# Gate logits' chunks one place earlier between the attention tiles, and the last modulation columns in another PSUM region

## What is computed

```python
def _hybrid_mixer(u, w_in, b_gate, ..., w_proj_att, w_proj_ssm, w_out):
    proj = u @ w_in
    q, k, v, us, g_att, g_ssm = jnp.split(proj, [...], axis=-1)
    for window, dilation in PATTERNS:
        o, lse = _dilated_window_attention(q, k, v, slopes, window, dilation)
...
    y_att = o_att @ w_proj_att
    y_ssm = _s5_branch(us, ...) @ w_proj_ssm
    merged = jax.nn.sigmoid(g_att + gb_att) * y_att + jax.nn.sigmoid(g_ssm + gb_ssm) * y_ssm
    return merged @ w_out
...
        mod = c_act @ w_ada[l] + b_ada[l]
        sh1, sc1, gt1, sh2, sc2, gt2 = jnp.split(mod, 6, axis=-1)
```

## Time and profile before

| | us |
|---|---|
| median of 3 runs | 1996.53 |
| lowest, highest | 1995.04, 1999.32 |
| the profiled execution's own time | 1995.31 |
| its span, first to last instruction | 1993.6 |
| TensorE busy | 1971.0 (99% of the span) |
| VectorE busy | 1143.7 (57%) |
| GpSimd busy | 1319.6 (66%) |
| ScalarE busy | 668.1 (34%) |

### The profile page before, as it was taken

How to read it: one execution, slowest core, us unless ns; L and a number is a source line. 1 busy time by engine, 2 the same in 40 slices (tenths; PEclk the granted TensorE clock), 3 DMA queues, 4 the chain that set the end, 5 groups by cost and what they waited for, 6 DMA issues and landing times. The chain is left out here.

```text
span 1993.6 us, 26010 instructions
## 1 busy us (share of the span) xinstructions
PE 1971.0 (99%) x10105; PEld 1639.9 (82%) x10105; DVE 1143.7 (57%) x1363; ACT 668.1 (34%) x1115; POOL 1319.6 (66%) x795
## 2 busy tenths in 40 slices
PE   8999999999999999999999999999999999999998
PEld 6888888888888787888888898888788888888888
DVE  6962378767652676656575386722464554624554
ACT  5213233233421454444321145433434433211103
POOL 4647457655364459999746538877787888858650
PEclk9999999999999999999999999999999999999999
DMA  9645564563644213333664422333323323198332
GB/s 336 201 118 160 172 185 151 159 199 115 216 161 156 85 64 106 103 130 106 234 251 159 148 86 64 119 115 112 120 77 136 127 85 106 34 377 317 117 137 86
DMA packets 195979, 295.41 MB, mean 148 GB/s; under 512 B 15416, under 2 KB 147472, under 8 KB 195856
## 3 DMA queue, kind: packets, MB, share of 16 engines
q1 hardware_dynamic: 185488, 270.55, 40.4%
q10 hardware_dynamic: 10368, 23.19, 3.1%
HBM read 213.73 MB, written 79.97 MB: 147 GB/s over the span
## 5 line engine op out<-in xcount | busy, mean ns | idle before, releaser
L1668 PE MATMUL ps<-tb,w_h 128*128 128x512 f32 x1344 | 416.9, 391 | 2.5 <-DVE quads L3056 1.9
L1052 POOL TENSOR_SCALAR w_h<-raw 128x512 fp32r<-128x512 f32 (+2 forms) x100 | 225.5, 2255 | 282.8 <-issue 127.1
L1173 POOL TENSOR_TENSOR w_l<-raw,w_h 128x512 fp32r<-128x512 f32 x210 | 309.5, 1483 | 92.6 <-ACT w_h L2307 92.6
L1668 PEld LDWEIGHTS ps<-tb,w_h 128*128 128x128 f32 x1344 | 251.3, 188 | 59.2 <-issue 3.9
L1668 PE MATMUL ps<-tb,w_l 128*128 128x512 f32 x672 | 261.5, 389 | 0.0
L2307 ACT ACTIVATE w_h<-raw 128x512 fp32r<-128x512 f32 x210 | 130.8, 627 | 236.8 <-PE ps L1668 150.3
L1668 PE MATMUL ps<-act_h,w_h 128*128 128x512 f32 x504 | 196.3, 389 | 0.6 <-ACT quads L2336 0.5
L1054 POOL TENSOR_TENSOR w_l<-raw,w_h 128x512 fp32r<-128x512 f32 (+2 forms) x100 | 191.3, 1913 | 8.3
L1668 PE MATMUL ps<-act_l,w_h 128*128 128x512 f32 x504 | 196.1, 389 | 0.0
L1668 PE MATMUL ps<-act_h,w_l 128*128 128x512 f32 x504 | 196.1, 389 | 0.0
L1668 PEld LDWEIGHTS ps<-tb,w_l 128*128 128x128 f32 x672 | 126.1, 188 | 26.3
(11 more groups left out here) (455 smaller groups left out, 4581.2 us busy)
## 6 DMA issues: line engine op xcount, KB each, us to landing
raw<-in_w_in SPq DMA_DIRECT2D x44, 1024.0 KB, 5.3
raw<-in_w_up SPq DMA_DIRECT2D x16, 1024.0 KB, 5.2
f_scratch<-r SPq DMA_DIRECT2D x16, 1024.0 KB, 8.3
gates_scratch<-quads SPq DMA_DIRECT2D x24, 512.0 KB, 7.6
r<-gates_scratch SPq DMA_DIRECT2D x12, 1024.0 KB, 6.4
ada_lo<-in_w_ada SPq DMA_DIRECT2D x16, 512.0 KB, 4.1
ada_hi<-in_w_ada SPq DMA_DIRECT2D x16, 512.0 KB, 4.4
gates_scratch<-gate_st ACTq DMA_DIRECT2D x32, 256.0 KB, 3.0
```

The source lines that it names most:

```text
L1052: nc.gpsimd.tensor_scalar(w_h[:, k, c, :], src[:, c, :], 1.0, None, ALU.mult).then_inc(s["w_high"], 1)
L1173: nc.gpsimd.tensor_tensor(w7_l[:, SLOTS[o]], x, w7_h[:, SLOTS[o]].bitcast(F32), ALU.subtract)\
L1668: last = nc.tensor.matmul(bank_of(n, bank), w[:, SLOTS[o], c, :], x(c), start=(first and c == 0 and p == 0), stop=(c == KD // 2 - 1 and p ...
```

## The change

Four edits, all on the attention stage and the step behind it. No instruction is added or taken away.

1. The chunks of the gates move one place forward: chunk 0 stands before the scores of the first two tiles, every `gate_part(i)` covers chunks 4i + 1 to 4i + 4 in place of 4i to 4i + 3, and the last tile has two chunks in place of three.
2. The last pair of modulation columns is written to the first two columns of slot 2, the transposes' region (`columns_of`), and TensorE no longer waits for `o_ready` and `mod2_ready` right before it.
3. The product that overwrites slot 3 now waits for `o_ready` and for the last but one read of columns. The one that overwrites slot 2 waits for the last read.
4. DVE reads the last pair of columns behind its last `o_low`.

```diff
+        def columns_of(k):
+            return slot(2)[:, 0:2] if k == NT // 4 - 1 else slot(3)[:, 2 * P:2 * P + 2]
...
             def gate_part(i):
 
-                gate_chunks(KD // 2 * i, KD // 2 * i + KD // 2)
+                gate_chunks(KD // 2 * i + 1, KD // 2 * i + KD // 2 + 1)
...
-                ada(slot(3)[:, 2 * P:2 * P + 2], ada_parts[k % 2]).then_inc(s["ada_done"], 1)
+                ada(columns_of(k), ada_parts[k % 2]).then_inc(s["ada_done"], 1)
...
+            pe.wait_ge(s["s5_act"], S5_ACT["sig_ready"] + 1)
+            gate_chunks(0, 1)
             for t in range(2):
                 scores(t)
-            pe.wait_ge(s["s5_act"], S5_ACT["sig_ready"] + 1)
-            gate_part(0)
+            gate_chunks(1, 5)
             scores(2)
...
                 else:
-                    gate_chunks(4 * KD * KD - 12 + 3 * (t - NT + 4), 4 * KD * KD - 9 + 3 * (t - NT + 4))
+                    at_g = 4 * KD * KD - 11 + 3 * (t - NT + 4)
+                    gate_chunks(at_g, min(at_g + 3, 4 * KD * KD))
...
             def last_columns_of_modulation():
 
-                pe.wait_ge(s["o_ready"], AHEAD + NT // 2)
-                pe.wait_ge(s["mod2_ready"], NT // 4 - 1)
                 modulation_columns(NT // 4 - 1)
...
                         pe.wait_ge(s["gate_read"], AHEAD + 4 * KD)
-                        pe.wait_ge(s["mod2_ready"], NT // 4)
+                        pe.wait_ge(s["o_ready"], AHEAD + NT // 2)
+                        pe.wait_ge(s["mod2_ready"], NT // 4 - 1)
...
                 if j == 0:
                     for cg in range(2):
+                        if cg:
+                            pe.wait_ge(s["mod2_ready"], NT // 4)
                         product(slot(2 * cg), N_PROJ % 2, cg, KA, o_h, o_l, each=None if cg else s["ot_ready"]).then_inc(s["gemm"], 2)
...
-                v.tensor_tensor(mod[:, lo:lo + 2], slot(3)[:, 2 * P:2 * P + 2], col_a("b_ada", lo, 2), ALU.add)\
+                v.tensor_tensor(mod[:, lo:lo + 2], columns_of(k), col_a("b_ada", lo, 2), ALU.add)\
                  .then_inc(s["mod2_ready"], 1)
...
-            modulation_read(NT // 4 - 1)
             normalised(NT // 4 - 1)
             for c in range(2, KA):
                 o_low(c)
+            modulation_read(NT // 4 - 1)
```

## The result

The changed kernel takes 2026.55 us (median of 5 runs, 2023.81 to 2030.01) against 1996.53 us before; the ratio is 1.0154, with a 95% interval of 1.0142 to 1.0167. It is slower by 30.0 us. Forecast were 2020.5 us, in a range of 2015.5 to 2027.5: the direction and the mechanism held, the size was 6 us short. The profiled execution took 2030.01 us, with a span of 2028.3 us, so it lies 3.5 us over the median.

What follows compares the result with a forecast made beforehand. TensorE, busy 1971.0 of 1993.6 us, was taken as the bound. 1995.3 + 33.3 - 5.2 - 3.9 - 0.2 = 2019.3 us, plus 1.2 to the median gave 2020.5 us, range 2015.5 to 2027.5.

Steps and rivals of the forecast that it cites:

- The exposed hand-over, 30 x 1.11 us: Attention stage: each group's first gate matmul waits uncovered for ScalarE's read of the bank, 1.57 - 0.46 us; 33.3 us added.
- ScalarE ready in time, with 1.15 us to spare: Gate hand-overs: ScalarE's read, due 0.69 us earlier, starts at once, as 1.15 of at least 1.84 us idle time remain.
- The old waits for the bank, 5.2 us won: Attention stage: 9 + 7 earlier TensorE waits for ScalarE's gate reads go; 5.2 us won, 4.4 to 5.4.
- The waits for VectorE's copy, 3.9 us won: Attention stage: five column-matmul waits for `prob_t` go because TensorE comes later; 3.9 us won, bounds 0 to 3.9.
- The start "at nothing": Start of attention stage: chunk 0 before the first scores costs nothing, being necessary work, with `w_split` no new wait.
- The columns, 0.2 us won: Modulation columns: TensorE's 0.42 us wait goes, but VectorE's chain ends only 0.18 us earlier; 0.2 us won, at most 1.4.
- rival (d): Gate hand-overs: short, frequent gaps lower TensorE's clock; up to 177 us, a tenth giving 2038 in all; chance 0.02.
- Nothing outside 217 to 545 us moves: Sign outside the attention stage: the forecast is wrong if anything there moves by more than 1 us.

Runs made afterwards that it cites:

- experiment 5: The kernel before with only the modulation-column edit (also spelled `e_columns_only`): 1994.53 us against 1994.10, ratio 1.0000.
- experiment 1: The changed kernel with chunk 0 put back behind the first two scores: 2023.58 us, ratio 1.0138 to the kernel before.
- experiment 6: The changed kernel with the next tile's transposes moved between a group's last chunk and the next group's first: 2013.18 us, ratio 1.0090 to the kernel before.
- experiment 2: The kernel before with only chunk 0 moved in front of the first scores: 1997.30 us against 1995.83, ratio 1.0009.
- experiment 3: The changed kernel with ScalarE reading each finished gate group twice before counting the bank as read: 2048.75 us.
- k_sums_moved_only: The kernel before with only one step of VectorE's modulation sums moved one tile later: 1996.24 us against 1996.22, ratio 0.9996.
- i_odd_tail_kept: The kernel before with the modulation edit and gate chunks shifted by four, three in each of the last four tiles, two in the two ahead: 1995.20 us, ratio 0.9998.

## Why the prediction was right and where it fell short

- **The exposed hand-over, 30 x 1.11 us: right.** 30 waits, distance 1.57 us in most. Summed over all thirty in the trace after, the distances are 47.6 us, less 30 x 0.46 = 33.8. Doubling the read and covering part of it moved the time as a fixed length on TensorE's path must. Against the stage of experiment 5, where the waits for VectorE are almost absent, the stage of experiment 1 is 322.36 - 294.98 = 27.4 us longer; 33.3 less the 5.2 for the old waits gives 28.1, less some 0.7 (an estimate: 0.4 and one slow restart) for the rest of VectorE's waits there 27.4.
- **ScalarE ready in time, with 1.15 us to spare: right.** 1.21 us were left in the hand-over shown, 1.15 at the least.
- **The old waits for the bank, 5.2 us won: right as far as it can be seen.** It stands in the same sum, which comes out; no run removes them alone.
- **The waits for VectorE's copy, 3.9 us won: right against the profiled execution, open for the usual run.** Without the start the stage is 322.36 - 297.98 = 24.4 us longer, 24.2 by the forecast. But that execution had more of these waits than another of the same order (2.5 us, against 0.4 in experiment 5, whose stage is 3.0 us shorter). A gain read from one execution was carried over to the median of all. Which stage is the usual one, the medians don't settle: experiment 6 at 19.1 us above before fits the shorter stage of experiment 5 better (19.7, against 16.7 with the other), experiment 2 at 1.5 us (interval 0.0 to 3.4) fits only the longer one (2.7, against 5.7). The reason given, that a later TensorE finds the copy done, was not tested by itself either. The rows show something beside it, which the forecast didn't look at: VectorE's sums, with 485 ns in the median, took up to 2.6 us each; those that the timelines of before and of experiment 5 list singly with more than 1.3 us all lie beside a GpSimd TENSOR_TENSOR. Two of them stand right before the copy of the earlier trace rows (GpSimd, then VectorE, in the trace of before):

```profile
345.63 2.96 POOL L1122 TENSOR_TENSOR k_ll<-k_ll,k_hh 128x1024 fp32r<-128x1024 f32 x1
...
346.72 3.40 DVE L2912 SCALAR_TENSOR_TENSOR ada_part<-ada_hi,c_act,ada_part 128x256 f32<-128x256 f32 x2
...
350.14 0.65 DVE L2864 COPY prob_t<-ps 128x512 f32<-128x512 f32 x1
```

In the stage after, the same 128 sums (L2910 and L2912 there, L2916 and L2918 here) took 71.8 us in place of 102.4. How the two engines' work falls together thus differs between the traces; no run here varied it by itself.
- **The start "at nothing": wrong, by 4.0 us.** The step that failed is "the weights of a group that starts earlier are loaded and split about a head ahead, so `w_split` is no new wait". That is true of every group but the first, which is the one that was moved ahead of its cover. In the code the first chunk of group 0 calls `split_done`, which waits for `w_split`, and the trace of before has the split's end 0.29 us ahead of the chunk. Reading those two rows would have given a wait of 218.96 - 217.39 = 1.6 us at least; the clock's fall behind a gap of 2.3 us or more could not be read from the stage. The price varies with the gap: 3.0 us of wait and 2.9 of clock in the trace of experiment 2.
- **The columns, 0.2 us won: nothing.** The stretch is 9.56 us with the change, 9.40 with that edit alone, 9.41 before. That TensorE would only wait longer for the last low half was right (1.3 and 1.1 us). The 0.18 us did not come back: from the start of VectorE's first low half there to that of the last two it is 4.26 us before (519.75 - 515.49) and 4.25 with the read gone (experiment 5, 516.89 - 512.64), since its neighbours took that much longer. Why is open.
- **The clock, rival (d): right for the short gaps, wrong in general.** It stayed up through thirty gaps of 0.86 us, and through those of 1.50 to 1.65 us in experiment 3. It fell behind the one of 1.93 us there, and in the changed kernel behind those of 2.00, 2.95 and 2.17 us.
- **"Nothing outside 217 to 545 us moves": not so in the profiles**, by 3.05 us ahead and 3.06 us behind, in code that didn't change. The first also shows in the profile of `k_sums_moved_only`, whose attention order is that of before, the second in that of `e_columns_only`. Each is a wait for VectorE that came out longer, by 0.33 and 1.1 us, with a fall of the clock behind it, and in the first the longer wait at 40 us. They come and go between kernels that are the same there, so I take them for variation between executions, which could account for the 3.5 us between this profile and the median. Why VectorE is later in some executions stays open.

Put together: 33.3 - 5.2 - 3.9 + 4.0 (start) = 28.2 us if a usual run pays VectorE's waits as the profiled one did, 33.3 - 5.2 - 0.7 + 4.0 = 31.4 if it pays them as the one of experiment 5. Measured were 30.0, with an interval of 28.4 to 33.3, so of the 6 us that were missing the start explains up to 4 (2.3 to 3.0 by the medians of experiment 1) and the rest is not assigned. That the time still fell into the range was in part luck: no bound held anything for the start, and its price fitted into the room left for other rivals, 1 us below the upper end.

## What to carry to other kernels

When work is moved ahead of other work, ask of the very first piece what it waits for, not only of the repeated pattern; the piece that moves to the front loses all of its cover. Where one PSUM bank is handed over between two engines, its price was here a nearly fixed distance (1.50 to 1.63 us at 29 of 30 places, 1.85 at one) that could be read before the change from any place where the wait already shows, and it was paid in full wherever the next group's first matmul directly followed the last. Before counting a gain at the end of a stage, look how early the next stage's operands land; the earlier end may only turn into another wait. Waits that come from two engines drifting against each other should be read in more than one execution before their removal is counted as a gain.

## What the runs showed of the hardware

TensorE's clock went to its lower level (1.2 GHz) behind single gaps. One of 2.95 us was followed by 3.4 us at half clock; in experiment 2, with 3.68 us, TensorE's first 5.9 us of work behind the gap ran at half. In experiment 3 the waits of up to 1.65 us left it at the upper level and the one of 1.93 us did not. Gaps near 2 us went either way: behind 2.09 us in `i_odd_tail_kept` (at 511.51 us) and 2.18 us in `k_sums_moved_only` (at 789.88 us) the clock stayed at 1.00. The 3 us behind the stage are the same thing. Before, and after, at the same unit of the feed-forward stage:

```profile
788.50 0.73 PE L1668 MATMUL ps<-tb,w_h 128*128 128x512 f32 x2 [1.06 <-DVE quads L3056]
...
821.18 1.04 PE L1674 MATMUL ps<-tb,w_h 128*128 128x512 f32 x2 [2.17 <-DVE quads L3062]
...
820.00:840.00 20.00, 18.82 (x76) 15.43 (x77) 16.43 (x15) 8.48 (x13) 14.80 (x9) 0.91 0.02 7
```

A wait that was 1.1 us longer took another 20 x 0.09 = 1.8 us of clock with it. So a gap of about 2 us cost up to nearly twice its idle time here (2.17 us idle and 1.8 of clock), and a kernel without a change to that place can show either.
